# Decay factors of the delta rule: subtraction, clamp and masks on VectorE instead of an absolute value on ScalarE and a mask on GpSimd

## The reference, cut to what matters

```
gcum  = cumsum(gc, axis=-1)
diff  = gcum[..., :, None] - gcum[..., None, :]
decay = where(tril, exp(where(tril, diff, 0.0)), 0.0)
a  = where(strict, einsum("bhncd,bhnsd->bhncs", kb, kc) * decay, 0.0)   # kb = k * beta
ia = a + eye            # solved for u and w
qk = where(tril, einsum("bhncd,bhnsd->bhncs", qc, kc) * decay, 0.0)
```

## Time and profile before

| | |
|---|---|
| time, median of 3 runs | 1605.54 us (1604.99 to 1606.22) |
| profiled execution: time, span | 1606.22 us, 1604.5 us |
| TensorE matmuls busy | 1487.3 us, 93% of the span |
| VectorE, ScalarE, GpSimd busy | 668.4, 513.0, 652.9 us |
| mean granted clock of TensorE | 0.970 of full speed |

### The profile page before, as it was taken

How to read it: one execution, slowest core, us unless ns; L and a number is a source line. 1 busy time by engine, 2 the same in 40 slices (tenths; PEclk the granted TensorE clock), 3 DMA queues, 4 the chain that set the end, 5 groups by cost and what they waited for, 6 DMA issues and landing times.

```text
span 1604.5 us, 20078 instructions
## 1 busy us (share of the span) xinstructions
PE 1487.3 (93%) x8186; PEld 1242.6 (77%) x8186; DVE 668.4 (42%) x1230; ACT 513.0 (32%) x874; POOL 652.9 (41%) x412
## 2 busy tenths in 40 slices
PE   5999987979899999999979989879898999999999
PEld 4888975657888888888868888756578888888887
DVE  6527457563333411343164374576534233114321
ACT  5442215443242222222235423153423232122320
POOL 4383133453334444344324722234622443444433
PEclk9999998999999999999989999979999999999999
DMA  6224120100423223332321421201002333333331
GB/s 164 81 66 113 27 53 1 27 1 1 85 79 102 82 92 105 105 92 86 98 75 60 112 67 27 53 1 27 1 5 76 98 86 99 98 105 86 99 99 72
DMA packets 182860, 112.67 MB, mean 70 GB/s; under 512 B 46576, under 2 KB 170480, under 8 KB 182768
## 3 DMA queue, kind: packets, MB, share of 16 engines
q1 hardware_dynamic: 182768, 111.39, 24.9%
HBM read 108.49 MB, written 2.88 MB: 69 GB/s over the span
## 4 chain that ended last, share of the span: by engine, by line
PE 79%; DVE 11%; issue 4%; POOL 4%; ACT 2%; DMA 0%; SPq 0%; ACTq 0%; POOLq 0%; DVEq 0%
PE ps L488 62%; PE ps L761 3%; PE ps L599 2%; PE ps L748 1%; PE ps L449 1%; DVE arena L256 1%; PE ps L768 1%; PE ps L527 1%; PE ps L731 1%; POOL arena L1248 1%; PE ps L732 1%; DVE arena L1431 1%; DVE hT_hi L1582 1%; DVE st L244 1%; PE ps L477 1%
## 5 line engine op out<-in xcount | busy, mean ns | idle before, releaser
L1154 POOL TENSOR_TENSOR w_lo<-w_raw,w_hi 128x2048 fp32r<-128x2048 f32 (+3 forms) x98 | 444.4, 4535 | 679.5 <-ACT w_hi L910 679.5
L910 ACT ACTIVATE w_hi<-w_raw 128x2048 fp32r<-128x2048 f32 (+1 forms) x100 | 188.8, 1888 | 609.8 <-PE ps L488 609.5
L488 PE MATMUL ps<-hT_hi,w_lo 128*128 128x512 f32 x928 | 235.7, 397 | 0.0
L488 PE MATMUL ps<-hT_hi,w_hi 128*128 128x512 f32 x896 | 223.3, 391 | 0.0
L488 PE MATMUL ps<-hT_lo,w_hi 128*128 128x512 f32 x896 | 222.3, 390 | 0.0
L488 PEld LDWEIGHTS ps<-hT_hi,w_lo 128*128 128x128 f32 x928 | 177.3, 192 | 37.1
L488 PEld LDWEIGHTS ps<-hT_lo,w_hi 128*128 128x128 f32 x896 | 167.6, 188 | 35.0 <-issue 0.3
L488 PEld LDWEIGHTS ps<-hT_hi,w_hi 128*128 128x128 f32 x896 | 166.9, 188 | 34.4 <-issue 0.3
L1665 DVE TENSOR_TENSOR aT_lo<-ffn_tmp,aT_hi 128x512 fp32r<-128x512 f32 x44 | 143.7, 3265 | 30.7 <-ACT aT_hi L919 30.7
L1714 DVE TENSOR_TENSOR ffn_tmp<-ps,ffn_tmp 128x512 f32<-128x512 f32 x44 | 30.4, 692 | 297.2 <-ACT ffn_tmp L1132 297.2
L488 PE MATMUL ps<-w_hi,aT_hi 128*128 128x512 f32 (+1 forms) x608 | 132.3, 345 | 0.0
(11 more groups left out here) (272 smaller groups left out, 1916.9 us busy)
## 6 DMA issues: line engine op xcount, KB each, us to landing
w_raw<-in_w_gate_up SPq DMA_DIRECT2D x88, 512.0 KB, 5.1
w_raw<-in_w_in SPq DMA_DIRECT2D x20, 1024.0 KB, 5.4
w_raw<-in_w_down SPq DMA_DIRECT2D x16, 1024.0 KB, 5.1
w_raw<-in_w_out SPq DMA_DIRECT2D x32, 256.0 KB, 4.4
w_raw<-in_w_down SPq DMA_DIRECT2D x8, 768.0 KB, 4.5
w_raw<-in_w_in SPq DMA_DIRECT2D x2, 1120.0 KB, 5.5
w_raw<-in_w_in SPq DMA_DIRECT2D x2, 1056.0 KB, 6.0
x_tok<-in_x SPq DMA_DIRECT2D x4, 512.0 KB, 5.3
```

The source lines that it names most:

```text
L488: mm = nc.tensor.matmul(out_ap, a(ab, k), b(bb, k), start=first and i == 0, stop=last and i == len(kts) - 1)
L910: nc.scalar.activation(whi[:, c % 2, 0:kt * w], raw[:, c % 2, 0:kt * w], ACT.Copy).then_inc(S["w_hi"], 1)
L1154: nc.gpsimd.tensor_tensor(wlo[:, c % 2, 0:kt * w], raw[:, c % 2, 0:kt * w], whi[:, c % 2, 0:kt * w].bitcast(F32), ALU.subtract).then_inc(S ...
```

## The change

The absolute value and the later mask of qkT go. VectorE now computes, for each head, two differences from bank 7: clamped at zero from below into dA (for L) and from above into dB (for qkT), which gives eight `tensor_scalar` of 128x128. ScalarE applies two `Exp` of 128x512, one to each. VectorE then multiplies dA by beta and by a new bf16 mask `below` (strictly lower triangle), dB by the mask `tri`, and at last four products with the PSUM banks write L and qkT. The semaphore `dabs` is replaced by `dec`, which VectorE raises after the eight differences; TensorE's line 581 and ScalarE wait for it. `qkmask` is gone. GpSimd makes the mask `below` once, at the start of the program.

```diff
@@ pool_setup
-            for t, v in ((ident, 0.0), (identb, 0.0), (tri, 1.0), (offblk, 1.0), (negm, 0.0),
+            for t, v in ((ident, 0.0), (identb, 0.0), (tri, 1.0), (below, 1.0), (offblk, 1.0), (negm, 0.0),
...
+            select(below[:], -1, [[-1, P]], 1, ALU.is_ge, 0.0)
@@ gdn_grams
-                    pe.wait_ge(*S.at("dabs", t, l))
+                    pe.wait_ge(*S.at("dec", t, l))
@@ recur_second
-                pe.wait_ge(*S.at("qkmask", 1, l))
@@ scalar_layer
-                    act.wait_ge(*S.at("gr", t + 1, l))
-                    if t:
-                        act.wait_ge(*S.at("dexp", t, l))
-                    for h in range(GH):
-                        i = nc.scalar.activation(dB[:, h, :], ps[:, 7, h * P:(h + 1) * P], ACT.Abs, scale=-1.0,
-                                                 bias=gsc[:, 2, t * GH + h:t * GH + h + 1])
-                    i.then_inc(S["dabs"], 1)
-                    act.wait_ge(*S.at("dabs", t + 1, l))
-                    if t:
-                        act.wait_ge(*S.at("A", t, l))
-                    nc.scalar.activation(dA, dB, ACT.Exp, scale=-1.0).then_inc(S["dexp"], 1)
+                    act.wait_ge(*S.at("dec", t + 1, l))
+                    nc.scalar.activation(dA, dA, ACT.Exp, scale=-1.0)
+                    nc.scalar.activation(dB, dB, ACT.Exp).then_inc(S["dexp"], 1)
@@ pool_layer
-            nc.gpsimd.affine_select(out=qkT, in_=qkT, compare_op=ALU.is_ge, fill=0.0, base=0,
-                                    pattern=[[0, NT * GH], [1, P]], channel_multiplier=-1).then_inc(S["qkmask"], 1)
@@ decays
+                dve.wait_ge(*S.at("gr", t + 1, l))
+                if t:
+                    dve.wait_ge(*S.at("A", t, l))
+                for h in range(GH):
+                    g0 = gsc[:, 2, t * GH + h:t * GH + h + 1]
+                    V.tensor_scalar(dA[:, h, :], ps[:, 7, h * P:(h + 1) * P], g0, 0.0, ALU.subtract, ALU.max)
+                    ins = V.tensor_scalar(dB[:, h, :], ps[:, 7, h * P:(h + 1) * P], g0, 0.0, ALU.subtract, ALU.min)
+                ins.then_inc(S["dec"], 1)
                 dve.wait_ge(*S.at("dexp", t + 1, l))
+                for h in range(GH):
+                    ins = V.scalar_tensor_tensor(out=dA[:, h, :], in0=dA[:, h, :], scalar=gsc[:, 1, t * GH + h:t * GH + h + 1],
+                                                 in1=below[:], op0=ALU.mult, op1=ALU.mult)
+                chain(V.tensor_tensor(dB, dB, tri[:].rearrange("p (o c) -> p o c", o=1).broadcast_to([P, GH, P]), ALU.mult))
                 dve.wait_ge(*S.at("gram", t + 1, l))
-                for h in range(GH):
-                    par, j = h % 2, h // 2
-                    V.scalar_tensor_tensor(out=L[:, t * GH + h, :], in0=ps[:, 3 + par, j * P:(j + 1) * P],
-                                           scalar=gsc[:, 1, t * GH + h:t * GH + h + 1], in1=dA[:, h, :],
-                                           op0=ALU.mult, op1=ALU.mult)
                 for par in range(2):
                     q0 = t * GH + par
-                    ins = V.tensor_tensor(qkT[:, q0:q0 + 3:2, :], ps[:, 5 + par, 0:256].rearrange("p (j c) -> p j c", j=2),
-                                          dA[:, par:par + 3:2, :], ALU.mult)
+                    for bank, dec, dst in ((3 + par, dA, L), (5 + par, dB, qkT)):
+                        ins = V.tensor_tensor(dst[:, q0:q0 + 3:2, :], ps[:, bank, 0:256].rearrange("p (j c) -> p j c", j=2),
+                                              dec[:, par:par + 3:2, :], ALU.mult)
                 ins.then_inc(S["A"], 1)
```

More of the change, by code:

```diff
@@ L57 @@
     "cfac": 1, "cmax": 1, "cmem": 1, "cmp": 3, "cmp_hid": 1, "cmp_kn": 1, "cmp_th": 1, "cmp_u": 1, "cmx": 1,
-    "conv": 6, "conv_w": 96, "cprob": 2, "cpt": 2, "csc": 2, "cy": 6, "d_in": 128, "d_out": 32, "dabs": 4, "dexp": 4,
+    "conv": 6, "conv_w": 96, "cprob": 2, "cpt": 2, "csc": 2, "cy": 6, "d_in": 128, "d_out": 32, "dec": 4, "dexp": 4,
     "ev_act": 24, "ev_dve": 10, "exp": 64, "g": 1, "gT": 6, "gback": 6, "gcum": 1, "geg": 1, "geg2": 1, "gexp": 1,
@@ L64 @@
     "norm_gains": 32, "oS": 4, "oall": 1, "og": 1, "ogT": 2, "ored": 1, "oseed": 1, "osq": 1, "pTa": 32, "pTd": 32,
[L65 to L69, removed]
+    "params": 160, "pscaled": 64, "ptr": 64, "pv": 64, "qdec": 1, "qhi": 8, "qkn": 1, "qlo": 4, "qn": 1, "qnT": 4,
+    "qnps": 4, "qps": 4, "qred": 4, "qrms": 1, "qseed": 1, "qsq": 4, "roped": 1, "scan": 1, "score": 48, "silu": 22,
+    "ssq1": 4, "ssq_next": 4, "state": 4, "szero": 1, "tdzero": 1, "tiinit": 1, "trig": 4, "up_mul": 22, "vbs": 1,
+    "vnew": 4, "w1": 32, "wS": 4, "w_hi": 50, "w_in0": 656, "w_in1": 656, "w_lo": 50, "x_down": 16, "x_res": 16,
+    "zth": 1,
 }
@@ L137, in trunk @@
         identb, negm = sb("identb", [P, P], BF16), sb("negm", [P, 2 * P], BF16)
-        offblk = sb("offblk", [P, P], BF16)
+        below, offblk = sb("below", [P, P], BF16), sb("offblk", [P, P], BF16)
         ones = sb("ones", [P, P])
```

## The result

The changed kernel takes 1624.63 us (median of 4 runs, 1622.77 to 1626.5) against 1605.88 us for the kernel before in the same comparison. The ratio is 1.0114, with a 95% interval of 1.0096 to 1.0133: slower by 18.8 us. Single executions spread: the changed kernel took 1622.8 to 1628.9 us in 12 of them, the kernel before, unchanged, 1603.0 to 1613.5 in all 67 on record here. The profiled execution took 1625.56 us with a span of 1623.8 us, 19.3 us more than before. The lines have moved: TensorE's by +1 (582 is the product for `gr`, 589 and 594 are the Gram products, 489 is the projection), those of GpSimd and VectorE by up to -10 (1159 the scalings, 1166 `trig`, 1146 the split).

A forecast was written before the change was run, and what follows sets the result against it. TensorE was taken to bound the kernel (79% of the chain), now waiting for VectorE's `A`. A delay of 8.0 us plus 0.3 for clock, 8.3 per layer, 16.6 over both, gave 1622 us, range 1611 to 1631.

The forecast's parts named there:

- The chain of one tile: From `gr` to `A`: VectorE, ScalarE, VectorE work sums to 6.48 us (5.0 to 7.9), over TensorE's round of 5.33.
- The hold: VectorE's five new operations per tile with two SBUF inputs wait for GpSimd's running instruction; those with a PSUM input don't.
- two cases: Layer 0, t = 0: `A` at 99.25 us if VectorE keeps its turn between `trig` operations, 101.6 if GpSimd interleaves; 101.6 taken.
- split's end + 2.98: Layer 0, t = 1: masks held until GpSimd's split ends near 106.9 us, then 2.98 us more, `A` at 109.9.
- The delay of the Gram products of t = 3: Layer 0: they wait for `A` of t = 2 at 116.4 us instead of starting at 108.45, 8.0 us late.
- GpSimd put off: VectorE's five operations of t = 0 take 1.5 us and delay the split's end from 105.46 to about 106.9 us.
- The clock inside the stage: TensorE's lower clock after its long wait costs 1.7 us, covered if at t = 1; 0.3 us added per layer.
- Behind the stage: After the Gram stage: transfers of L and `w1` come 2.7 us later against TensorE, but `w1` still lands before it is wanted.
- I put the tail at nothing: Work after the Gram stage: no added cost; 0.4 us with the longest chain.
- No hold: Rival in the stage: GpSimd does not hold the new SBUF operations; 3.5 us per layer, 1612 us; chance 10%.
- fits in 5.33: Rival in the stage: the chain fits into TensorE's 5.33 us round; delay 0, 1605.5 us stands; chance 5%.
- The heavier form: Rival in the stage: chain 7.9 us, plus clock and tail costs; 12.3 us per layer, 1630 us; chance 9%.

The follow-up runs named there:

- experiment 5: The kernel before with the square of the compressed keys (line 1347) reading one factor from PSUM instead of both from SBUF: 1605.3 us, ratio 0.9993.
- experiment 1: The changed kernel without beta, the mask of dA and the mask of dB (five VectorE operations per tile): 1607.43 us, ratio 0.9999.
- Experiments 7 and 8: The kernel before: with line 1347's square reading PSUM and GpSimd's first split delayed, 1603.81 us; with 2 more passes of eight projection products per layer, 1616.14 us.
- experiments 8 to 10: The kernel before with 2, 4 or 7 more passes of eight projection products ahead of group 11 in each layer: 1616.14, 1615.54 and 1621.08 us.
- experiment 2: The changed kernel with the GpSimd split that held the masks of t = 1 moved behind the fourth `gr`: 1623.45 us, ratio 1.0088.

## Why the prediction was right, point by point

The prediction was 1622 us (1611 to 1631), slower, by a chain that no longer fits under TensorE's round. It came out at 1624.6. The mechanism was the one named, and TensorE waited at the six places named. The size is in part luck: two terms of the sum were off and partly cancel. The stage cost 12.6 us and not 16.6, and a cost of 7.0 us stood where I had put nothing.

**The chain of one tile: 6.48 us predicted, 6.58 measured** at t = 2. The eight differences took 2.16 us (2.18), the two Exp 1.16 (1.20), the mask of dB 0.68 (0.69), the four products 1.41 (1.45). Only the four masks were mis-sized: 1.14 us instead of 0.80. I had reckoned that an operation in SBUF might start the next one sooner than one with PSUM; it doesn't, one starts every 0.26 us in both. "VectorE: DVE Perf Modes" in the Trainium skill, section "The DRAIN you can't avoid", has the next operation start only once the pipe is empty, and one that is not held earlier. The trace shows the second case: at full length, eight differences would take eight times 0.343 = 2.75 us, and they took 2.16.

**The hold: right.** The masks, with all inputs in SBUF, were held (2.98 and 3.91 us for four), the operations with an input in PSUM weren't, and experiment 5 shows it on one operation.
- At t = 0 I had two cases and took the one in which GpSimd puts an operation between each of VectorE's. The other one came true: after the scalings' end (95.54) it took 3.21 us to `A` at 98.75, against 2.98 and 5.3 predicted. As I had said, it made no difference to what followed.
- At t = 1 the reckoning was "split's end + 2.98". Measured: 105.21 to 108.21, 3.00 us; in layer 1 910.56 to 913.55, 2.99 us.
- At t = 2 it was 6.68 us more (108.21 to 114.89), against 6.48.

**The delay of the Gram products of t = 3: 8.0 us predicted, 6.49 measured in layer 0 and 6.07 more in layer 1.** I had them near 116.5 us, and they came at 114.94. The split ended at 105.21 instead of 106.9: GpSimd began 0.7 us earlier than in the kernel before (89.92 for 90.64), and was put off by 0.5 us instead of 1.5. The longer chain and the handovers added 0.2 us: 8.0 - 1.7 + 0.2 = 6.5. The stages by themselves grew by 8.71 and 6.07. They differ by when GpSimd's work comes beside TensorE's. The scalings end 5.31 us after the Gram products of t = 0 in layer 0 and 2.54 us in layer 1, and were 3.82 in the kernel before, from which I reckoned. What moved them is in the main the clock. TensorE has one wait of 3.03 us, at line 572 (now 573), before the stage, in both kernels. In the kernel before a stretch at 0.57 followed it in layer 0 and one at 0.61 in layer 1. In the changed kernel, in layer 0 and then in layer 1:

```profile
78.42 0.40 PE L573 MATMUL ps<-gsc,tri 128*128 128x16 f32 x2 [3.03 <-DVE gsc L1377]
...
79.71 1.19 PE L489 MATMUL ps<-w_hi,hT_hi 128*128 128x256 f32 x8
...
883.61 0.61 PE L573 MATMUL ps<-gsc,tri 128*128 128x16 f32 x2 [3.03 <-DVE gsc L1377]
...
886.09 2.06 PE L489 MATMUL ps<-w_hi,hT_hi 128*128 128x256 f32 x8
```

Eight products of 256 columns take 1.19 us after the wait in layer 0, which is the time at full clock, and 2.06 us in layer 1. So the changed kernel reaches the stage 2.2 us earlier in layer 0 (the Gram products of t = 0 at 90.23 for 92.45 us): 0.7 of them it already had ahead at the wait's end (78.42 for 79.12), and 1.5 come behind it. I had taken as the rule, a 3 us wait followed by a stretch at half clock; it is only one of the outcomes.

**GpSimd put off: less than reckoned.** I had added the 1.5 us of VectorE's five operations. The eight `trig` operations took 5.15 us beside them, against 4.65 where the masks are out (experiment 1), so 0.5 us in layer 0. By "SBUF — State Buffer" in the Trainium skill, section "SBUF: two separate sides", whichever of the two engines starts first has the shared ports for its whole instruction, and the other waits. The trace agrees in sign, with 0.5 us.

**The clock inside the stage: as reckoned, in effect.** The wait of 3.18 us at t = 1 was followed by a granted clock of 0.50 (100 to 104 us), and it was covered: TensorE still waited for `A` 1.45 us at t = 2. So not even the 0.3 us that I had added are seen.

**Behind the stage: right for the transfers, wrong for the clock.** The stretch to the first narrow product grew by 0.02 us: `w1` was issued by 128.82 and TensorE began at 135.80 with no wait. The solve's first operation was held for 1.90 instead of 3.85 us, and the hold by the old mask (1.70 us) was gone, as I had said; its slack grew:

```profile
128.90 1.90 DVE L1421 TENSOR_TENSOR arena<-arena 128x1 f32<-128x1 f32 x1 [7.33 <-DMA arena<-diag_in]
...
148.06 0.33 DVE L1320 COPY peb<-ps 64x1 f32<-64x1 f32 x2 [3.74 <-PE ps L532]
```

It was 1.44 us in the earlier trace rows; 1.3 us of the growth only mean that VectorE waited for a slower group of narrow products (3.49 for 2.18 us). **The step that failed is "I put the tail at nothing".** It looked for waits alone. The tail has none, but it has a piece whose length depends on the granted clock, and that piece grew by 3.4 and 3.6 us. Experiments 7 and 8 have the slow form in kernels with an undisturbed stage as well. Why it comes is not shown (experiments 8 to 10), and so it is not shown that the change brings it about. That all 12 executions of the changed kernel lie 4 us or more above 1605.9 + 12.6 = 1618.5 speaks for a cost that comes with it each time. One profile of the kernel before could not have told it.

**The rivals.** "No hold" and "fits in 5.33" are refuted by the masks' durations and by the six waits; experiment 2, where the masks are hardly held, has the Gram products of t = 3 3.9 us later than the kernel before in layer 0 (112.31 for 108.45), where that rival had 3.5. The heavier form was wrong in its chain (6.58, not 7.9), and the time lies above the forecast for another reason, the 7.0 us behind the stage.

## What to carry to other kernels

Compare the length of a helper's chain with the period of the engine that it serves, not with its idle share: VectorE was idle for more than half of the time, and 3 us more per tile still cost over 1%. Where GpSimd works in SBUF at that time, leave one input of a VectorE operation in PSUM, or expect the operation to last until GpSimd's is done; and if GpSimd's instruction is moved instead, look for the next VectorE operation that it will hold. Do not put a difference of some 3 us per place down to a cause before the same matmuls have been compared at the same clock, and in more than one execution: here a stretch without gaps took 16.3 or 20.2 us in two kernels that reached it at the same time. And compare absolute times beside lengths: a stage can be longer only because it was reached earlier.

## What was not expected of the hardware

- The same gap-free sequence of TensorE (128 narrow products and 24 wide ones) took from 16.3 to 21.0 us over these kernels: 16.3 to 16.6 or about 20 in most, 18.0 to 18.2 in three places. How long the granted clock stays at half there varies, with nothing in the instructions of the stretch to tell it.
- The same wait of 3.03 us was followed by a stretch at half clock in three of the four places in the kernels before and after, and by none in the fourth (layer 0 of the changed kernel, where eight products of 256 columns took 1.19 us).
- A `tensor_scalar` on 31x2 numbers in SBUF was held for 3.93 us beside a GpSimd split, while the `tensor_reduce` of 31x128 just before it took 0.27 us beside the same split.
- Between GpSimd operations that stand in a row, a waiting VectorE operation gets through: the first mask of t = 0 ended 0.15 us after the scaling that it had waited for, though GpSimd was busy without a gap.
